# Hybrid conv / differential-attention trunk with MoE: order of the first loads, ScalarE's first table, and the place of the output bias

## The chip, the cores and the metric
One core of one Trainium2 chip. The metric is the device time of one launch in microseconds, median of several runs. The profile shows one execution, whose own time stands beside its span.

## The reference, cut to what matters
```python
for i in range(2):                          # layer 0: conformer_conv, layer 1: diff_attention
    x = x + mixer(rms_norm(x, norm1_g[i]))
    x = x + hierarchical_moe(rms_norm(x, norm2_g[i]), ...)   # 32 experts, group top-1, expert top-2

def conformer_conv(h, w_in, b_in, dw, dw_b, ln_g, ln_b, w_out, b_out):
    u = h @ w_in + b_in                     # (512,1024) @ (1024,2048)
    a, g = jnp.split(u, 2, axis=-1)
    u = a * jax.nn.sigmoid(g)
    u = causal_depthwise_conv(u, dw) + dw_b # 31 taps, each channel by itself
    u = jax.nn.silu(layer_norm(u, ln_g, ln_b))
    return u @ w_out + b_out                # (512,1024) @ (1024,1024)
```
x is 1 x 512 x 1024 float32, and so are all parameters and the output. An expert has three weight matrices of 2 MB each.

## The kernel before, in words
One program gives each engine its own instruction list; the lists meet at semaphores. x lives in `x_res` as 4 row tiles of 128 x 1024. Weights come in "units" of 2 MB (two DMAs of 1 MB, all issued by SP) into a ring of 6 buffers, and in the MoE into four more areas.

SP's list begins with the four x tiles (`L403`), the first norm gain (`L405`), units 0 and 1 (first halves of the two column groups of `w_in`, `L316` inside `mix_unit`), then six small loads into `chan_rows`: the 31 rows of the depthwise taps (`L409`), three vectors of one row (`L411`), the input bias as two rows (`L412`), and `b_out` (`L413`). Then come units 2 and 3 (the other halves of `w_in`), 4 and 5 (`w_out`), and small parameters of later stages. After that SP waits: MoE units 0 and 1 may be loaded once four groups of `w_in` columns are multiplied (`glu_ready` 4), two more at `glu_ready` 8, then at `mix_ready` 4, `mix_ready` 8 and so on.

GpSimd's list begins with constants, one after the other, and ends that part with `consts_ready` (`L508`). ScalarE, VectorE and TensorE wait for it. ScalarE (`L625`, `L626`, `L631`) then makes the row norms of the four x tiles: square and sum, root, scale. TensorE transposes the scaled tile (`L1168`), and VectorE multiplies by the gain into `hT` (`L830`). TensorE next waits for all six small loads, transposes `chan_rows` (36 rows, `L1189`), VectorE copies the result to `chan` (`L845`) and counts `chan_taken`. Only then does TensorE start the `w_in` product (`L1180`).

The convolution runs over 8 groups `ct` of 128 channels. For each, TensorE makes 16 accumulating matmuls (the profile counts 32 pieces), ScalarE the gate's sigmoid (`L646`), VectorE the gated product (`L853`). Taps 0 to 11 are multiplied by ScalarE (`L659`) and summed by GpSimd (11 adds, `L518`), taps 12 to 30 go to VectorE (`L870`, `L873`), and VectorE joins both sums (`L881`, `L882`) into `uT`, which lies in `area2`. On ScalarE the gate of group ct+1 stands after the seventh tap product of group ct. Layer-norm sums (`L1195`) come from TensorE, the rest of the layer norm is on VectorE and ScalarE.

`mix_out` multiplies `uT` by `w_out` in 8 pieces of output (2 column halves x 4 row tiles), 8 matmuls each (16 pieces in the profile, `L1231`). For layer 0 each ends with one more matmul, ones times `b_out` (`L1234`), that adds the bias. VectorE adds each result to `x_res` (`add_mix`, `L902`); from the fifth on, norm, transposes and router logits follow for the row tile.
Of the kernel before, what the change touches and what calls it, by code (L numbers as in the profile page):

```python
# [27 lines left out]
ALU = mybir.AluOpType  # L28
ACT = mybir.ActivationFunctionType
# [36 lines left out]
def trunk(nc, x, norm1_g, norm2_g, conv_w_in, conv_b_in, conv_dw, conv_dw_b, conv_ln_g, conv_ln_b,  # L66
# [11 lines left out]
    with ctx:  # L78
# [50 lines left out]


        consts_ready, params_loaded, x_loaded = sem("consts_ready"), sem("params_loaded"), [sem(f"x_loaded{t}") for t in range(NT)]
        gain_loaded, route_loaded = sem("gain_loaded"), sem("route_loaded")
# [12 lines left out]
        tap_made, tap_added, conv_done, sq_done = sem("tap_made"), sem("tap_added"), sem("conv_done"), sem("sq_done")  # L145
        stats_ready, ln_var, ln_std, ln_x, ln_done = sem("stats_ready"), sem("ln_var"), sem("ln_std"), sem("ln_x"), sem("ln_done")
        mix_ready, mix_taken = sem("mix_ready"), sem("mix_taken")

# [62 lines left out]
        chan_rows = area3[0:TAPS + 5, 0:D]  # L211
        b_out = area3[0:1, 3072:3072 + D]
        PAD = TAPS - 1
# [98 lines left out]
        def _(sp):  # L312
# [89 lines left out]
            for t in range(NT):  # L402
                sp.dma_start(x_res[:, t, :], x[0, t * P:(t + 1) * P, :]).then_inc(x_loaded[t], 16)  # L403
                if t == 0:
                    sp.dma_start(norm_g[:, 0, :], norm1_g[0].rearrange("(h p j) -> p h j", h=2, j=4)).then_inc(gain_loaded, 16)  # L405
            mix_unit(0, cols_dram(w_in, 0))
            mix_unit(1, cols_dram(w_in, D))

            sp.dma_start(chan_rows[0:TAPS, :], conv_dw[0]).then_inc(params_loaded, 16)  # L409
            for r, vec in enumerate((conv_dw_b, conv_ln_g, conv_ln_b)):  # L410
                sp.dma_start(chan_rows[TAPS + r:TAPS + r + 1, :], vec).then_inc(params_loaded, 16)  # L411
            sp.dma_start(chan_rows[TAPS + 3:TAPS + 5, :], conv_b_in[0].rearrange("(r n) -> r n", r=2)).then_inc(params_loaded, 16)  # L412
            sp.dma_start(b_out, conv_b_out).then_inc(params_loaded, 16)  # L413
            mix_unit(2, cols_dram(w_in, 512))
# [56 lines left out]
        def _(pool):  # L471
# [3 lines left out]
            def link(ins):  # L475
# [3 lines left out]
                pool.wait_ge(pool_chain, linked[0])  # L479

            link(g.memset(ones[:], 1.0))
            link(g.memset(eps[:], EPS))
            for half in range(2):
# [24 lines left out]
            g.memset(step_count[:], 0.0).then_inc(consts_ready, 1)  # L508


            k = 0
# [96 lines left out]
        def _(act):  # L608
# [8 lines left out]

            act.wait_ge(consts_ready, 1)

# [192 lines left out]
        def _(dve):  # L812
# [44 lines left out]
            for ct in range(NC):  # L857
# [4 lines left out]
                for k, w in enumerate(range(POOL_TAPS, TAPS)):  # L862
                    acc = sums[k % 2]
                    dst = uT[:, ct, :] if w == TAPS - 1 else acc
                    if k >= 2:
                        dve.wait_ge(dve_taps, k0 + k - 1)
                    elif ct >= 1:
                        dve.wait_ge(conv_done, ct)
                    if k < 2:
                        ins = v.tensor_scalar(acc, ub[:, w:w + T], chan[:, ct, w:w + 1],  # L870
                                              chan[:, ct, TAPS:TAPS + 1] if k == 0 else 0.0, ALU.mult, ALU.add)
                    else:
                        ins = v.scalar_tensor_tensor(dst, ub[:, w:w + T], chan[:, ct, w:w + 1], acc, ALU.mult, ALU.add)  # L873
                    ins.then_inc(dve_taps, 1)
# [19 lines left out]

            def add_mix(l):

                for n in range(2):
# [260 lines left out]
        def _(pe):  # L1158
# [25 lines left out]
            for t in range(NT):  # L1184
                transpose_xn(N_PRE[0], t)
            pe.wait_ge(params_loaded, 16 * 6)
            R = TAPS + 5
            for ct in range(NC):
                last = nc.tensor.transpose(bank[5][:, ct * R:(ct + 1) * R], chan_rows[:, ct * P:(ct + 1) * P], ident[0:R, 0:R])  # L1189
            last.then_inc(chan_ready, 1)  # L1190


            def stats(ct):
                pe.wait_ge(sq_done, ct + 1)
                mm(bank[4][:], ones[:], uT[:, ct, :], start=ct == 0, stop=ct == NC - 1)  # L1195
                return mm(bank[5][:], ones[:], sq_ct[:, ct, :], start=ct == 0, stop=ct == NC - 1)

            pe.wait_ge(xt_taken, 8)
            pe.wait_ge(chan_taken, 1)
            for ct in range(NC):  # L1200
# [7 lines left out]
                last = project(bank[2 * (ct % 2) + 1][:], w_chunks(ug), hT, cols)  # L1208
                last.then_inc(glu_ready, 1)
                if ct >= 3:  # L1210
                    stats(ct - 3)
# [3 lines left out]

            def mix_out(l, n0, src, bias):

# [3 lines left out]
                for n in range(2):  # L1221
                    for t in range(NT):
# [4 lines left out]
                        for c in range(NC - 1 if k < ahead[l] else 0, NC):  # L1227
                            if k == 0:

                                pe.wait_ge((ln_done, oT_done)[l], c + 1)  # L1230
                            last = mm(dst[:], src[:, c, t * P:(t + 1) * P], w_chunks(n0 + n)[:, c, :],  # L1231
                                      start=c == 0, stop=c == NC - 1 and not bias)
                        if bias:
                            last = mm(dst[:], ones[0:1, :], b_out[:, n * 512:(n + 1) * 512], start=False, stop=True)  # L1234
                        last.then_inc(mix_ready, 1)
# [140 lines left out]

            mix_out(0, 4, uT, True)
            route(0)
# [111 lines left out]
            for h, g, e in attention_steps():  # L1490
# [49 lines left out]
                if h is not None:  # L1540
                    v_half(h, 1)
            mix_out(1, n0 + 6, oT, False)
            route(1)
# [25 lines left out]
```

## Time and profile before
| | |
|---|---|
| median of 3 runs | 1679.39 us (1675.87, 1679.39, 1686.95) |
| the profiled execution | 1679.18 us, span 1677.3 us |
| TensorE busy | 1391.7 us, 83% |
| VectorE, ScalarE, GpSimd busy | 459.1, 333.1, 276.7 us |
| DMA | 473.12 MB, mean 282 GB/s |

The profiled execution's time is its span and 1.9 us around it. Times within the profile count from the start of the span. An engine's name with a q (SPq) is its sequencer: there DMAs are issued.

### The profile page before, as it was taken

The numbers are of one execution on the slowest core, as the hardware profiler recorded it, in microseconds if no ns is written. First come the engines' busy times: TensorE is split into PE (matmuls) and PEld (weight loads), VectorE is DVE, ScalarE is ACT, GpSimd is POOL, SyncE is SP. The second block draws the span as 40 slices with busy tenths as digits, with TensorE's granted clock in tenths as the row PEclk, the third lists the DMA queues.
The fourth block names the chain that finished last, engine by engine and source line by source line (L and its number), as shares of the span: only waits on it lengthen the run. The fifth ranks groups of instructions, "written<-read, shape, count | busy, mean of one in ns | idle before, by whom it ended". The sixth has DMA issues, their size and how long they took to land.

```text
span 1677.3 us, 16737 instructions
## 1 busy us (share of the span) xinstructions
PE 1391.7 (83%) x5868; PEld 623.2 (37%) x5868; DVE 459.1 (27%) x868; ACT 333.1 (20%) x629; POOL 276.7 (16%) x380
## 2 busy tenths in 40 slices
PE   4996596998778788887599999996998778778783
PEld 2442144333223232232365675644333223223231
DVE  1699714111011010110444454424111011011012
ACT  3466311110000000000334444421100000000000
POOL 1688200211111111111000000000121111111110
PEclk9998698999999999999699999996999999999997
DMA  9122015899999999999700400326899999999994
GB/s 340 25 100 100 1 67 234 345 363 419 420 421 420 420 420 419 418 417 352 269 1 1 150 1 23 129 83 239 357 382 420 421 420 420 419 419 412 419 410 183
DMA packets 91248, 473.12 MB, mean 282 GB/s; under 512 B 19675, under 2 KB 19675, under 8 KB 40260
## 3 DMA queue, kind: packets, MB, share of 16 engines
q1 hardware_dynamic: 78500, 443.12, 65.2%
q0 software_dynamic: 10400, 16.82, 2.7%
q10 hardware_dynamic: 2304, 12.58, 1.9%
q8 instruction: 28, 0.46, 0.1%
q14 instruction: 16, 0.13, 0.0%
HBM read 466.43 MB, written 23.33 MB: 292 GB/s over the span
## 4 chain that ended last, share of the span: by engine, by line
PE 48%; DMA 34%; DVE 8%; POOL 4%; SPq 3%; issue 3%; ACT 2%; ACTq 0%; POOLq 0%; DVEq 0%
DMA ring<-in_moe_w 31%; PE banks L1287 19%; PE banks L1397 5%; PE banks L1231 5%; POOL scratch L518 4%; PE banks L1304 3%; PE banks L1426 3%; SPq L316 2%; PE banks L1180 2%; DVE banks L873 2%; PE banks L1486 1%; PE banks L1441 1%; DMA area<-y_dram 1%; DMA area<-in_conv_b_out 1%; PE banks L1468 1%
## 5 line engine op out<-in xcount | busy, mean ns | idle before, releaser
L1287 PE MATMUL banks<-ring,scratch 128*64 128x512 f32 x1984 | 498.2, 653 | 145.8 <-DMA ring<-in_moe_w 134.0
L1287 PEld LDWEIGHTS banks<-ring,scratch 128*64 128x64 f32 x1984 | 159.1, 149 | 481.2 <-issue 481.2
L1015 DVE COPY scratch<-banks 128x256 f32<-128x256 f32 x65 | 27.6, 425 | 799.9 <-PE banks L1295 799.9
L1304 PE MATMUL banks<-ring,scratch 128*64 128x512 f32 x1008 | 230.2, 598 | 3.0 <-DVE scratch L1015 3.0
L687 ACT ACTIVATE scratch<-banks 64x512 f32<-64x512 f32 x65 | 38.2, 588 | 598.1 <-PE banks L1287 598.1
L536 POOL COPY at_out<-rows_out 128x1 int32 (+1 forms) x64 | 11.6, 181 | 698.1 <-ACT scratch L691 698.1
L518 POOL TENSOR_TENSOR scratch<-scratch 128x512 f32<-128x512 f32 x88 | 111.8, 1271 | 61.3 <-ACT scratch L659 50.0
L1397 PE MATMUL banks<-hT,ring 128*128 128x512 f32 x256 | 117.9, 604 | 0.9 <-DVE hT L830 0.9
L1180 PE MATMUL banks<-hT,ring 128*128 128x512 f32 x256 | 113.0, 602 | 0.7 <-issue 0.7
L1304 PEld LDWEIGHTS banks<-ring,scratch 128*64 128x64 f32 x1008 | 68.1, 136 | 117.3 <-issue 110.3
L1231 PE MATMUL banks<-ring,area 128*128 128x512 f32 x200 | 91.3, 609 | 10.6 <-ACT area L669 9.6
L691 ACT ACTIVATE scratch<-banks 128x512 f32<-128x512 f32 x65 | 38.8, 597 | 284.4 <-PE banks L1304 284.4
L873 DVE SCALAR_TENSOR_TENSOR banks<-scratch,chan,banks 128x512 f32<-128x512 f32 x128 | 85.0, 750 | 0.0
L659 ACT ACTIVATE scratch<-scratch,chan 128x512 f32<-128x512 f32 x96 | 66.7, 718 | 48.3 <-POOL scratch L518 34.5
L539 POOL DMA_INDIRECT y_dram<-scratch,at_out x64 | 65.3, 1020 | 56.5 <-POOL at_out L536 56.5
L1180 PEld LDWEIGHTS banks<-hT,ring 128*128 128x128 f32 x256 | 49.4, 194 | 63.0 <-issue 63.0
L546 POOL MEMSET scratch<- 128x512 f32 x4 | 2.1, 524 | 425.3 <-DVE x_res L902 425.2
L528 POOL DMA_INDIRECT scratch<-xn_dram,at_in x60 | 63.1, 1051 | 53.8 <-POOL at_in L525 48.5
L1397 PEld LDWEIGHTS banks<-hT,ring 128*128 128x128 f32 x256 | 46.2, 189 | 49.4 <-issue 46.9
L1426 PEld LDWEIGHTS banks<-ring,hT 128*128 128x128 f32 x512 | 59.0, 192 | 3.8 <-issue 3.8
L1231 PEld LDWEIGHTS banks<-ring,area 128*128 128x128 f32 x200 | 37.6, 194 | 61.0 <-issue 56.1
L1426 PE MATMUL banks<-ring,hT 128*128 128x128 f32 x512 | 59.6, 275 | 0.0
(208 smaller groups left out, 1142.6 us busy)
## 6 DMA issues: line engine op xcount, KB each, us to landing
ring<-in_moe_w SPq DMA_DIRECT2D x374, 1024.0 KB, 16.7
area<-in_moe_w SPq DMA_DIRECT2D x12, 1024.0 KB, 11.1
ring<-in_attn_w_qkv SPq DMA_DIRECT2D x12, 1024.0 KB, 10.8
ring<-in_conv_w_in SPq DMA_DIRECT2D x8, 1024.0 KB
area<-y_dram ACTq DMA_DIRECT2D x8, 1024.0 KB, 8.0
ring<-in_conv_w_out SPq DMA_DIRECT2D x4, 1024.0 KB, 12.9
xn_dram<-area ACTq DMA_DIRECT2D x8, 512.0 KB, 2.7
hT<-in_moe_w SPq DMA_DIRECT2D x4, 1024.0 KB, 7.6
```

Of the source, the lines that this page charges most:

```text
L518: g.tensor_tensor(pacc[ct % 2], pacc[ct % 2], tap[(k - 1) % TAP_BUFS], ALU.add).then_inc(tap_added, 1)
L528: g.indirect_dma_start(out=xe[s], out_offset=None, in_=xn_dram[l][:, :], in_offset=bass.IndirectOffsetOnAxis(ap=at_in[:, s:s + 1], axis=0) ...
L539: g.indirect_dma_start(out=y_dram[l][:, :], out_offset=bass.IndirectOffsetOnAxis(ap=at_out[:, s:s + 1], axis=0), in_=y_sb[s], in_offset=No ...
L659: a.activation(dst, u_buf[ct % 2][:, w:w + T], ACT.Copy, scale=chan[:, ct, w:w + 1]).then_inc(tap_made, 1)
L691: a.activation(y_sb[s], bank[6 + s][:], ACT.Copy).then_inc(sems["y_taken"], 1)
L873: ins = v.scalar_tensor_tensor(dst, ub[:, w:w + T], chan[:, ct, w:w + 1], acc, ALU.mult, ALU.add)
L1180: last = mm(dst, w[:, c, cols], src[:, c, :], start=start and c == 0, stop=stop and c == NC - 1)
L1231: last = mm(dst[:], src[:, c, t * P:(t + 1) * P], w_chunks(n0 + n)[:, c, :], start=c == 0, stop=c == NC - 1 and not bias)
L1287: last = mm(bank[2 + s][q * SLOTS:(q + 1) * SLOTS, :], xeT[s][:, j, h, :], w[:, c, :], start=c == 0, stop=c == NC - 1)
L1304: last = mm(bank[6 + s][q * SLOTS:(q + 1) * SLOTS, :], hidT[s][:, j, :], w2c[:, j, q * 512:(q + 1) * 512], start=j == 0, stop=j == 3)
L1397: last = mm(qk_bank[c][:], w_chunks(u)[:, k, (h % 4) * P:(h % 4 + 1) * P], hT[:, k, :], start=k == 0, stop=k == NC - 1)
L1426: last = mm(v_bank[:, t * P:(t + 1) * P], hT[:, k, t * P:(t + 1) * P], w_chunks(u)[:, k, (h % 4) * P:(h % 4 + 1) * P], start=k == 0, stop= ...
```

## The change
- SP loads the parameters ahead of units 0 and 1, not behind them. The 31 tap rows come as 16 and 15 rows; each of the five vectors comes as 16 parts of 64 numbers. Then SP waits until unit 1 has landed, loads the output bias broadcast to 128 partitions (`b_wide`, in `area2`), and only then units 2 to 5.
- TensorE no longer transposes `chan_rows` ahead of the `w_in` product but after its first group (`columns()`), and waits for `chan_taken` only at group 3.
- ScalarE no longer waits for all of GpSimd's constants but for `eps` alone, which GpSimd now writes first, and runs one root of `eps` before anything else.
- GpSimd adds `b_wide` to each tile of `x_res` once the tile's norm is taken (4 additions of 128 x 1024), ahead of its first tap sum. The bias matmul of `mix_out` is gone. VectorE waits for `bias_added` before the last two taps of group 0 and in `add_mix`.

```diff
@@ SP
+            for lo, hi in ((0, 16), (16, TAPS)):
+                sp.dma_start(chan_rows[lo:hi, :], conv_dw[0, lo:hi]).then_inc(params_loaded, 16)
+            parts = lambda ap: ap.rearrange("r (a n) -> r a n", a=16)
+            for r, vec in enumerate((conv_dw_b, conv_ln_g, conv_ln_b, conv_b_in[:, 0:D], conv_b_in[:, D:2 * D])):
+                sp.dma_start(parts(chan_rows[TAPS + r:TAPS + r + 1, :]), parts(vec)).then_inc(params_loaded, 16)
             mix_unit(0, cols_dram(w_in, 0))
             mix_unit(1, cols_dram(w_in, D))
-            sp.dma_start(chan_rows[0:TAPS, :], conv_dw[0]).then_inc(params_loaded, 16)
-            for r, vec in enumerate((conv_dw_b, conv_ln_g, conv_ln_b)):
-                sp.dma_start(chan_rows[TAPS + r:TAPS + r + 1, :], vec).then_inc(params_loaded, 16)
-            sp.dma_start(chan_rows[TAPS + 3:TAPS + 5, :], conv_b_in[0].rearrange("(r n) -> r n", r=2)).then_inc(params_loaded, 16)
-            sp.dma_start(b_out, conv_b_out).then_inc(params_loaded, 16)
+            loaded(sp, 1)
+            sp.dma_start(b_wide, conv_b_out.to_broadcast([P, D])).then_inc(bias_loaded, 16)
             mix_unit(2, cols_dram(w_in, 512))
@@ GpSimd
+            g.memset(eps[:], EPS).then_inc(eps_ready, 1)
             link(g.memset(ones[:], 1.0))
-            link(g.memset(eps[:], EPS))
...
+            pool.wait_ge(bias_loaded, 16)
+            for t in range(NT):
+                pool.wait_ge(xn_done, t + 1)
+                g.tensor_tensor(x_res[:, t, :], x_res[:, t, :], b_wide, ALU.add).then_inc(bias_added, 1)
@@ ScalarE
-            act.wait_ge(consts_ready, 1)
+            act.wait_ge(eps_ready, 1)
+            link(a.activation(small_at(21), eps[:], ACT.Sqrt))
@@ VectorE, taps and add_mix
+                    if ct == 0 and w >= TAPS - 2:
+                        dve.wait_ge(bias_added, NT)
...
+                if l == 0:
+                    dve.wait_ge(bias_added, NT)
@@ TensorE
-            pe.wait_ge(params_loaded, 16 * 6)
-            R = TAPS + 5
-            for ct in range(NC):
-                last = nc.tensor.transpose(bank[5][:, ct * R:(ct + 1) * R], chan_rows[:, ct * P:(ct + 1) * P], ident[0:R, 0:R])
-            last.then_inc(chan_ready, 1)
+            def columns():
+                pe.wait_ge(params_loaded, 16 * 7)
+                R = TAPS + 5
+                for ct in range(NC):
+                    last = nc.tensor.transpose(bank[5][:, ct * R:(ct + 1) * R], chan_rows[:, ct * P:(ct + 1) * P], ident[0:R, 0:R])
+                last.then_inc(chan_ready, 1)
             pe.wait_ge(xt_taken, 8)
-            pe.wait_ge(chan_taken, 1)
...
                 last.then_inc(glu_ready, 1)
+                if ct == 0:
+                    columns()
+                if ct == 3:
+                    pe.wait_ge(chan_taken, 1)
@@ mix_out
-                                      start=c == 0, stop=c == NC - 1 and not bias)
-                        if bias:
-                            last = mm(dst[:], ones[0:1, :], b_out[:, n * 512:(n + 1) * 512], start=False, stop=True)
+                                      start=c == 0, stop=c == NC - 1)
```

## Rows read from the trace of the kernel before

**Rows 1.** The page, chain that ended last: shares of the span.
```profile
PE 48%; DMA 34%; DVE 8%; POOL 4%; SPq 3%; issue 3%; ACT 2%; ACTq 0%; POOLq 0%; DVEq 0%
```

**Rows 2.** Chain in order of time, 0 to 72 us: start, length, what.
```profile
14.77 13.92 DMA area<-in_conv_b_out
28.73 1.06 PE banks L1189 x8
29.80 0.72 issue
30.52 29.97 PE banks L1180 x64
60.51 0.69 ACT scratch L646
...
61.89 1.28 POOL scratch L518
```

**Rows 3.** Timeline, 0 to 30 us: start, length, engine, what, [idle <-releaser].
```profile
4.13 1.28 ACT L625 ACT_TABLE_LOAD   x1 [4.13 <-DMA x_res<-in_x]
...
6.53 1.06 ACT L625 ACTIVATE scratch<-x_res 128x1024 f32<-128x1024 f32 x1 [1.12 <-POOL step_count L508]
...
7.70 1.28 ACT L626 ACT_TABLE_LOAD   x1
...
10.68 1.04 ACT L625 ACTIVATE scratch<-x_res 128x1024 f32<-128x1024 f32 x1
...
10.91 1.95 PE L1168 MATMUL banks<-ident,area 128*128 128x128 f32 x8 [10.91 <-ACT area L631]
...
13.89 0.25 SPq L411 DMA_DIRECT2D area<-in_conv_ln_g  x1
...
21.08 0.69 DVE L830 TENSOR_TENSOR hT<-banks,norm_g 128x512 f32<-128x512 f32 x1 [0.16 <-PE banks L1168]
...
29.83 0.46 DVE L845 COPY chan<-banks 128x288 f32<-128x288 f32 x1 [8.06 <-PE banks L1189]
```

**Rows 4.** Timeline, 44 to 70 us, same columns.
```profile
46.82 1.28 ACT L646 ACT_TABLE_LOAD   x1 [27.82 <-PE banks L1180]
48.12 0.69 ACT L646 ACTIVATE scratch<-banks,chan 128x512 f32<-128x512 f32 x1
48.84 0.75 DVE L853 SCALAR_TENSOR_TENSOR scratch<-banks,chan,scratch 128x512 f32<-128x512 f32 x1 [18.42 <-ACT scratch L646]
51.04 8.34 POOL L518 TENSOR_TENSOR scratch<-scratch 128x512 f32<-128x512 f32 x6 [44.54 <-ACT scratch L659]
...
56.03 0.25 SPq L432 DMA_DIRECT2D b_route<-in_moe_b_exp  x1
60.51 0.69 ACT L646 ACTIVATE scratch<-banks,chan 128x512 f32<-128x512 f32 x1 [4.61 <-PE banks L1180]
61.89 8.16 POOL L518 TENSOR_TENSOR scratch<-scratch 128x512 f32<-128x512 f32 x6 [2.51 <-ACT scratch L659]
68.92 0.70 DVE L881 TENSOR_TENSOR banks<-scratch,banks 128x512 f32<-128x512 f32 x1 [5.98 <-POOL scratch L518]
```

**Rows 5.** Chain in order of time, layer 0's output product and after.
```profile
213.18 1.05 PE banks L1234 x2
214.23 7.06 PE banks L1231 x16
221.29 1.05 PE banks L1234 x2
...
246.69 1.16 PE banks L1168 x8
247.85 6.87 PE banks L1231 x16
...
359.42 0.33 SPq L316
...
360.83 15.30 DMA ring<-in_moe_w
```

**Rows 6.** SP's waits, 200 to 480 us: total, times, longest.
```profile
SPq L316 <- PE banks L1234: 114.5, 2, 78.7
SPq L316 <- PE banks L1287: 102.7, 13, 11.6
```

**Rows 7.** Core by stretch: busy time and count, then PEclk, DMA share, GB/s.
```profile
0.00:19.50 19.50, 6.36 (x26) 5.19 (x27) 4.32 (x10) 12.60 (x18) 4.28 (x30) 1.00 0.91 323
20.00:28.70 8.70, 1.04 (x5) 0.64 (x3) 1.38 (x2) 0.00 (x0) 0.00 (x0) 1.00 1.05 354
8.00:20.00 12.00, 6.86 (x29) 5.69 (x30) 4.32 (x10) 9.87 (x15) 0.00 (x0) 1.00 1.04 391
30.50:35.00 4.50, 4.48 (x6) 1.92 (x7) 0.00 (x0) 0.00 (x0) 0.00 (x0) 1.00 0.95 351
35.00:60.00 25.00, 25.00 (x60) 11.13 (x59) 11.12 (x17) 6.70 (x9) 7.61 (x6) 1.00 0.51 145
```

**Rows 8.** DMA between 46.5 and 52 us: totals.
```profile
DMA packets 1127, 0.19 MB, mean 35 GB/s; under 512 B 1098, under 2 KB 1098, under 8 KB 1127
```

**Rows 9.** Tile x_res, 0 to 60 us: the four x loads.
```profile
DMA to landing us min/median/max: 3.3/6.1/7.3
```

**Rows 10.** Chain in order of time, layer 1's output product, which has no bias.
```profile
1119.21 0.95 PE banks L1168 x8
1120.16 6.87 PE banks L1231 x16
```

**Rows 11.** Tile ring, 0 to 90 us: durations min/median/max in ns, first and last start.
```profile
L316 SPq DMA_DIRECT2D ring<-in_moe_w x4: 355/426/647, 88.0 to 89.3; - x4
```

More of the change, by code:

```diff
@@ L128, in trunk @@
         ssq, std, rstd = small_at(0, NT), small_at(4, NT), small_at(8, NT)
+        eps_ready = sem("eps_ready")
         consts_ready, params_loaded, x_loaded = sem("consts_ready"), sem("params_loaded"), [sem(f"x_loaded{t}") for t in range(NT)]
@@ L146, in trunk @@
         stats_ready, ln_var, ln_std, ln_x, ln_done = sem("stats_ready"), sem("ln_var"), sem("ln_std"), sem("ln_x"), sem("ln_done")
+        bias_loaded, bias_added = sem("bias_loaded"), sem("bias_added")
         mix_ready, mix_taken = sem("mix_ready"), sem("mix_taken")
@@ L211, in trunk @@
         chan_rows = area3[0:TAPS + 5, 0:D]
-        b_out = area3[0:1, 3072:3072 + D]
+        b_wide = area2[:, 0:D]
         PAD = TAPS - 1
@@ L1214, in _, with mix_out @@
             stats(NC - 1).then_inc(stats_ready, 1)
-            def mix_out(l, n0, src, bias):
+            def mix_out(l, n0, src):
                 for n in range(2):
@@ L1375, in experts @@
                         down(o, 0, unit(n1 + 2), j + 1).then_inc(o["y_ready"], 1)
-            mix_out(0, 4, uT, True)
+            mix_out(0, 4, uT)
             route(0)
@@ L1541, in _ @@
                     v_half(h, 1)
-            mix_out(1, n0 + 6, oT, False)
+            mix_out(1, n0 + 6, oT)
             route(1)
```

## Prediction
> **What bounds the kernel now.** I read the page's chain first: TensorE has 48% of it and DMA 34% [rows 1], so no one engine bounds the whole, and the question is which wait ends last in the two stages that the change touches. Next, the chain in order of time. It runs through the last small load, `b_out`: issued at 14.77, landed 13.92 us later, at 28.69. Only then come the transposes of `chan_rows`, VectorE's copy, and the first `w_in` matmul at 30.52 [rows 2, 3]. The norm was long ready: the last piece of `hT` ends at 21.77 [rows 3]. So the wait for parameters costs up to 8.7 us in front of the convolution. From 30.52 TensorE does two groups in 29.97 us, ScalarE's second gate follows at 60.51, and from there GpSimd's adds carry the chain [rows 2, 4]. After the convolution the output product is a pure TensorE chain: 8.11 us for one piece of output, of which 1.05 is the bias matmul [rows 5].
>
> What follows is the MoE, bound first by TensorE and, from 359 us on, by weight loads that SP issues when TensorE frees a buffer [rows 5]. SP there waits on TensorE, two long waits on the output product and 13 on the experts' first products [rows 6]. No such wait ends by itself, so what the head saves should move the whole rest forward.
>
> **Why the parameters come late.** x and units 0 and 1 are 4 x 0.524 + 4 x 1.049 = 6.29 MB. The cores' DMA moved 323 GB/s over the first 19.5 us, which is 6.30 MB [rows 7]: the bytes of units 0 and 1 are in at 19.5 us. The six small loads hold 37 rows of 4 KB, 0.15 MB, yet need another 9 us, at 16 GB/s, while all DMA engines together do 354 in that stretch [rows 7]. That looks like one of 16 engines working the rows off one by one, at about 9.2 / 37 = 0.25 us a row, beside its share of units 2 and 3. The Trainium skill gives a reason (DMA: Bandwidth & Descriptors, "Why a DMA increments its semaphore by 16 and not by 1"): a load is split over the largest number of engines up to 16 that divides its outer dimension, so 31 rows go to one engine. This trace agrees, with those 16 GB/s. By that rule the new 16 and 15 rows use 16 and 15 engines, and the vectors' 16 parts use 16.
>
> **The change part by part.**
>
> *Parameters first, TensorE's start.* The same 0.15 MB now stands ahead of units 0 and 1. At the full rate of 391 GB/s [rows 7] it costs 0.4 us. At the rate of the stretch with many small loads, 35 GB/s [rows 8], it would cost 4.3. 127 of 147 KB are full 4 KB rows, so I take 0.6. SP needs 7 issues of 0.25 us plus gaps [rows 3], about 2 us, ahead of the units; x keeps the DMA engines busy meanwhile (it is a third of the 6.3 MB), so this is hidden. Without that cover it would cost those 2 us. From the last byte to the semaphore I take 0.9 us: the quickest x load landed 3.3 us after its issue [rows 9], of which its 0.524 MB need 1.3 to 1.8 us, so start and end share 1.5 to 2.0. Units 0 and 1 are then there at 19.5 + 0.6 + 0.9 = 21.0, and TensorE starts at 21.0, not at 30.52: 9.5 us earlier. Bounds: 20.0 and 25.5.
>
> *ScalarE's early table and the shorter wait for constants.* Now a table load, a wait for GpSimd until 6.53 and a second table load of 1.28 stand in the first tile's norm [rows 3]. With the table there and only `eps` to wait for, the square starts when x arrives, at about 4.1. VectorE still needs the constants at about 6.5, so the second tile starts near 7.8 where it started at 10.68 [rows 3], 2.9 earlier, and `hT` is ready near 18.9. The weights land at 21.0. So this edit is worth nothing by itself; it is cover that keeps `hT` (21.77 before) from being 0.8 us late. Priced at 0, but without it the start would be 21.8.
>
> *The transposes of `chan_rows`.* Before, 1.06 + 0.72 us stood in front of the product. That is already in the 9.5. Now they stand between groups 0 and 1. There the clock should be at its high level, where eight transposes of the x kind take 0.95 to 1.16 us [rows 5, 10] against 1.95 at the low level [rows 3]; the small ones took 1.06 at the low level [rows 2], so I take 0.7 on TensorE's path (bounds 0.5 and 1.1).
>
> *The clock of the start.* In the first 4.5 us of the product only 6 pieces ran (some 0.8 us each), after 35 us 60 pieces in 25 us (0.42 each) [rows 7]: the low level, 1.2 GHz, then the high one, 2.4 GHz. (PEclk reads 1.00 in both rows; the pieces speak against that for the first.) Its transposes before that (6.86 us of the 12 up to 20 [rows 7]) did not bring it up. I take the same slow start; if the rise comes up to 2 us sooner or later, half of that is gained or lost, 1 us.
>
> *The first gate.* Group 0 takes 46.8 - 30.5 = 16.3 us, so `glu_ready` 1 comes at 37.3, `chan_taken` at 37.3 + 0.7 + 0.5 (the copy [rows 3]) + 0.1 = 38.6. ScalarE's table load of 1.28 us starts on `glu_ready`, as at 46.82 [rows 4]; at 4.13 a table load ran although GpSimd's wait was still open [rows 3], so it will be hidden behind `chan_taken` (if not: 1.2 us, and see the slack next). The sigmoid is then at 38.7 instead of 48.12, the gated product at 39.4, the first GpSimd add due at 41.6 instead of 51.04: 9.4 earlier.
>
> *The second gate, which carries the chain.* TensorE reaches `glu_ready` 2 at 21.0 + 29.97 + 0.7 = 51.7, against 60.49: 8.8 us earlier. GpSimd was idle 2.51 us for that gate and VectorE then 5.98 us for GpSimd [rows 4], and with both ends moved by 9.4 and 8.8 the order stays. I take **8.8 us** for the convolution. Groups 1 to 7 repeat unchanged.
>
> *GpSimd's bias additions.* SP wakes at 21.0, the 0.5 MB broadcast needs 0.4 (issue), 1.3 (at 391 GB/s) and about 1.5 us (start and end): landed at 24.3. Four additions of 128 x 1024 at twice the 1.28 us of a 128 x 512 one [rows 2] are 10.2 us: done at 34.5. Behind them on GpSimd stand only the tap adds, due at 41.6, and then 2.5 us of idle time: 9 us of cover. At 35 GB/s [rows 8] the broadcast would take 15 us, landed near 38, and the additions end at 48: 3.3 us late. VectorE's new waits for `bias_added` are over long before its last two taps of group 0, near 51; the wait in `add_mix` costs nothing.
>
> *Units 2 to 5 held back.* From 22.7 on, 8.4 MB at 354 to 391 GB/s, in by 48. Unit 3 is wanted for group 4: SP's wait for group 3's end let MoE loads go at 88.0 before [rows 11], so near 79 now. Units 4 and 5 are wanted long after that. The last of the small loads behind them on SP is issued at 56 before [rows 4] and near 65 now, still ahead of SP's wait that ends near 79. No cost; the cover is 14 us or more.
>
> *The bias matmul gone.* It is on the chain eight times, once in each piece. It took 1.05 us, and the piece after it 7.06 where after transposes it is 6.87 (layer 0 and layer 1 alike), and the transposes after it 1.16 where layer 1 without bias shows 0.95 [rows 5, 10]. So 8 x 1.05 + 7 x 0.2 = **9.8 us**. Lower bound 8 x 1.05 = 8.4. VectorE and ScalarE between the pieces have 6.87 us for under 4 us of work, so TensorE stays last.
>
> Sum: 8.8 + 9.8 = 18.6 us, 1679.2 - 18.6 = 1660.6 for the profiled execution. Its time lies 0.2 below the median of the runs, so the same holds for that: 1660.8.
>
> **The rivals.**
> 1. *Dear small loads or a late bias.* The 0.15 MB ahead of the weights at 35 GB/s [rows 8]: start at 24.7, gain 14.9, 1664.5. The late broadcast: gain 15.3, 1664.1; both together about 1667. For it speaks that small loads do run that slowly in the one stretch that has them; against it, that most bytes here come in 4 KB rows and that x covers the issues. The Trainium skill speaks on this side (DMA: Bandwidth & Descriptors): transfers under 64 KB are dominated by their descriptors, and pieces under 512 B are written by read-modify-write. No row here has 256 B pieces alone.
> 2. *The spread does not happen*: the 15 rows, or all, go to one engine again. Then that engine has up to 15 x 0.25 = 3.8 us more than the others ahead of its share of the units, and `loaded` waits for the slowest: gain 15, 1664.4; with all 36 rows' worth on one engine 9 us late, gain 9.8, 1669.6. No row shows such a split of rows or parts, for it or against it; that x, with 128 rows, comes at nearly the full rate of all engines [rows 7] makes me hold the spread for likely.
> 3. *The gain is taken back*: clock phases in the MoE or weight loads that do not move forward. With only one of the two gains kept, 1669 to 1670. Against it: every wait of SP there is on TensorE [rows 6].
> 4. *Slower.* The one mechanism is GpSimd's queue: everything in the convolution hangs on the tap adds, and the bias additions now stand ahead of them behind SP, a landing and a broadcast. It costs 1 us for each us that the bias lands after 34.5 and outweighs the gain from 53 on; slower by 1% from about 70. At the lowest rate in sight it lands at 38, so this needs a broadcast three times slower still. At 75 us: 1679.2 - 18.6 + 40 = 1701.
>
> **How the numbers follow.** The forecast has a chance of 55%, rival 1 18%, rival 2 10%, rival 3 12%, rival 4 5%. About 1% is what a measurement of this kernel can tell from no change (the three runs lie 0.7% apart). 1% is 16.8 us, so that line lies at 1662.6, only 2 us above the forecast. Of the forecast's 55%, the clock and the scatter of the runs put about 10 behind the line; rivals 1 to 3 lie behind it by 1.5 us or more, and the same scatter puts about 10 of their 40 before it. So: faster by over 1% 0.55, within 1% 0.40, slower 0.05. Range: down to 1653 (TensorE starts at 20.0, the clock rises early, and 5 us of scatter), up to 1671 (rivals 1 to 3 with a little scatter). It leaves out rival 4 and the far ends of the others, less than 2 in 10.
>
> **What would show it.** `L1180` begins at 21 (20 to 25.5) and no longer waits for a parameter; `L1189` after the first 32 pieces; GpSimd's four additions between 24 and 35, with tap adds from 41.6; second gate near 51.7; 16 `L1234` pieces gone and output pieces every 6.9 us; x tile 2 squared near 7.8; MoE weights' first wait on SP 18 us earlier and the same total DMA. Wrong would be: the first product waiting on `ring` beyond 23; GpSimd waiting on `b_wide` after 34; a clock that stays at the low level in group 1.

## The result and the profile after

| | before | after |
|---|---|---|
| median | 1680.36 us (4 runs, 1675.87 to 1686.95) | 1665.59 us (4 runs, 1663.20 to 1667.35) |
| profiled execution | 1679.18 us, span 1677.3 | 1667.35 us, span 1665.6 |
| ratio | | 0.9915, 95% interval 0.9889 to 0.9941 |

The change saves 14.8 us, 0.85%; 18.6 were forecast. The two profiled executions lie only 11.8 us apart: that of after was the slowest of its four runs. So two things are to be explained: what the head and the output product gave, and where the profiles lost more than the medians.

The chain in order of time of after, first 75 us; compare [rows 2]:

```profile
8.14 13.65 DMA ring<-in_conv_w_in
21.79 0.14 issue
21.93 16.41 PE banks L1193 x32
38.33 0.62 PE banks L1209 x8
38.95 13.94 PE banks L1193 x32
52.90 0.02 issue
52.92 0.69 ACT scratch L655
...
54.29 1.28 POOL scratch L526
```

The parameters are gone from the chain. It now runs through units 0 and 1, which land at 21.8, and TensorE starts at 21.93 (30.52 before). The transposes of `chan_rows` stand after group 0 and cost 0.62. The second gate comes at 52.92 (60.51 before). The timeline of after shows the rest of the head, with [rows 3, 4]:

```profile
4.32 1.06 ACT L634 ACTIVATE scratch<-x_res 128x1024 f32<-128x1024 f32 x1 [2.03 <-DMA x_res<-in_x]
...
18.07 0.69 DVE L839 TENSOR_TENSOR hT<-banks,norm_g 128x512 f32<-128x512 f32 x1 [0.16 <-PE banks L1181]
21.81 0.37 SPq L416 DMA_DIRECT2D area<-in_conv_b_out  x1
21.93 16.41 PE L1193 MATMUL banks<-hT,ring 128*128 128x512 f32 x32 [3.90 <-DMA ring<-in_conv_w_in]
...
26.39 9.23 POOL L517 TENSOR_TENSOR x_res<-x_res,area 128x1024 f32<-128x1024 f32 x4 [20.02 <-DMA area<-in_conv_b_out]
...
42.63 8.34 POOL L526 TENSOR_TENSOR scratch<-scratch 128x512 f32<-128x512 f32 x6 [7.00 <-ACT scratch L668]
```

`hT` ends at 18.76, 3.2 us ahead of the weights. The four bias additions end at 35.62 and GpSimd then idles 7.00 us, so they are hidden.

The chain through the output product and into the router, after, with [rows 5]:

```profile
230.76 0.95 PE banks L1181 x8
231.72 6.87 PE banks L1248 x16
...
248.69 0.70 DVE x_res L915
...
252.32 1.98 PE banks L1181 x8
254.30 3.26 PE banks L1265 x16
...
258.13 3.56 PE banks L1265 x16
...
278.06 5.96 PE banks L1188 x8
...
285.43 13.95 PE banks L1302 x64
```

and the same stretch of before:

```profile
267.13 0.70 DVE x_res L902
...
270.76 1.23 PE banks L1168 x8
271.98 1.71 PE banks L1250 x16
...
274.03 1.91 PE banks L1250 x16
...
292.09 4.77 PE banks L1175 x8
...
298.27 13.95 PE banks L1287 x64
```

Most output pieces take 6.87 us. The last addition to `x_res` begins at 248.69 instead of 267.13: 18.4 us are saved there, nearly all that was forecast. But the first expert begins at 285.43 instead of 298.27, only 12.8 us earlier. In between, the same transposes take 1.98 us instead of 1.23, the same 16 logit pieces 3.26 and 3.56 instead of 1.71 and 1.91, and the 8 filler pieces that the kernel has there anyway 5.96 instead of 4.77. The rows by stretch say why (the columns are those of [rows 7]); first after, then before:

```profile
251.60:252.30 0.70, 0.05 (x1) 0.00 (x0) 0.67 (x2) 0.67 (x1) 0.00 (x0) 0.86 1.05 445
252.30:262.00 9.70, 9.68 (x44) 9.47 (x44) 1.38 (x2) 1.28 (x1) 0.00 (x0) 0.50 0.99 398
```
```profile
270.80:276.30 5.50, 5.47 (x44) 5.22 (x44) 1.29 (x2) 1.28 (x1) 0.00 (x0) 1.00 1.01 384
```

The same 44 pieces ran at a granted clock of 0.50, which is 1.2 GHz, and at 1.00, which is 2.4 GHz. Just before them TensorE waits for the last row tile's norm. Timeline of after, TensorE:

```profile
252.32 1.98 PE L1181 MATMUL banks<-ident,area 128*128 128x128 f32 x8 [0.68 <-DVE hT L839]
```

The question for the experiments was whether the change brings the low clock about. Their texts call two answers theory A (where the clock falls differs from execution to execution) and theory B (it falls there because the output product now ends without bias matmuls). A "filler" is a matmul by the identity whose result nobody reads.

### The profile page after: what moved, and what is told of

Same layout as the page of the kernel before. It is cut to its first block, busy times and chain, and to the rows that moved or that the text cites. A ratio compares the mean times of both kernels' runs of the same rounds, so it can differ in the third digit from the quotient of the medians.

```text
span 1665.6 us, 16714 instructions
## 1 busy us (share of the span) xinstructions
PE 1386.0 (83%) x5852; PEld 625.3 (38%) x5852; DVE 459.0 (28%) x868; ACT 332.0 (20%) x629; POOL 285.9 (17%) x384
## 4 chain that ended last, share of the span: by engine, by line
PE 48%; DMA 34%; DVE 8%; POOL 4%; issue 3%; SPq 2%; ACT 2%; ACTq 0%; POOLq 0%; DVEq 0%
DMA ring<-in_moe_w 32%; PE banks L1302 19%; PE banks L1412 5%; PE banks L1248 5%; POOL scratch L526 4%; PE banks L1319 3%; PE banks L1441 3%; SPq L318 2%; PE banks L1193 2%; DVE banks L884 2%; PE banks L1501 2%; PE banks L1456 1%; DMA area<-y_dram 1%; PE banks L1265 1%; PE banks L1483 1%
## 5 line engine op out<-in xcount | busy, mean ns | idle before, releaser
L1248 PE MATMUL banks<-ring,area 128*128 128x512 f32 x200 | 90.0, 608 | 10.6 <-ACT area L678 9.6
## 6 DMA issues: line engine op xcount, KB each, us to landing
ring<-in_attn_w_qkv SPq DMA_DIRECT2D x12, 1024.0 KB, 13.6
```

## The experiments

They ran in three groups: e0 to e2 and e6, then e3 to e5 and e7, then e8 to e11. Each ratio is to the kernel before in the same group (its medians 1681.24, 1679.18 and 1681.84 us), with its 95% interval.

| run | median us | ratio | interval |
|---|---|---|---|
| e0 changed kernel again | 1664.75 | 0.9912 | 0.9889 to 0.9936 |
| e1 loads and table only | 1671.57 | 0.9936 | 0.9913 to 0.9959 |
| e2 bias only | 1670.45 | 0.9937 | 0.9914 to 0.9960 |
| e6 changed + filler | 1659.47 | 0.9867 | 0.9842 to 0.9892 |
| e3 late table | 1662.40 | 0.9898 | 0.9876 to 0.9919 |
| e4 no hold | 1662.09 | 0.9893 | 0.9868 to 0.9918 |
| e5 no spread | 1670.11 | 0.9935 | 0.9911 to 0.9958 |
| e7 more fillers | 1661.35 | 0.9895 | 0.9873 to 0.9916 |
| e8 before + filler | 1679.55 | 0.9985 | 0.9970 to 1.0001 |
| e9 filler, no hold | 1657.55 | 0.9860 | 0.9841 to 0.9880 |
| e10 as e6 | 1660.29 | 0.9879 | 0.9860 to 0.9899 |
| e11 as e7 | 1660.89 | 0.9882 | 0.9866 to 0.9899 |

What the profiles add, read the same way in each: start of the first `w_in` matmul; then for each layer the time from the start of VectorE's last addition to `x_res` until the first expert's matmul, and how long after that addition the granted clock fell.

```
run      w_in starts  layer 0: stage, clock falls after   layer 1: stage, clock falls after
before     30.52         31.1      10.3                      36.9       3.8
after      21.93         36.7       3.4                      36.9       3.9
e0         22.98         35.3       4.0                      35.3       4.0
e1         22.07         35.3       4.1                      36.9       3.9
e2         30.57         36.7       3.4                      36.9       3.9
e3         21.73         33.7       6.0                      36.9       3.8
e4         22.73         35.2       3.9                      36.9       3.7
e5         27.82         35.3       4.0                      35.3       4.3
e6         22.93         33.6      10.8                      33.5      10.6
e7         22.21         32.4      10.0                      32.0      11.0
e8         30.22         33.7      10.8                      33.5      10.7
e9         22.50         33.1       9.5                      32.0      11.1
e10        22.18         33.5      10.7                      33.3      10.3
e11        23.30         32.4      10.8                      32.2      10.9
```

### The halves of the change, and the clock (e0, e1, e2, e6)

e0 is the changed kernel. 

> The changed kernel once more, unedited. Theory A (what is missing from the forecast was lost to the granted clock after the output product of layer 0): where the clock falls is not the same in each execution, so a new profile may show the logits of layer 0 at either speed (16 pieces in 1.71 us or 3.3 to 3.6 us); the median stays at 0.991 of before. Rival theory B (the fall belongs to this kernel, because its output product ends without the bias matmuls): the fall comes within 4 us of the last output piece again, and the experts begin 13 us earlier than before, not 18.

Measured: 0.9912 again. The clock fell 4.0 us after the addition, and the first expert begins at 285.64, 12.6 us earlier than before, which are theory B's numbers.

e1 puts the bias back on TensorE; GpSimd's additions and the waits for them are taken out:
```diff
-            sp.dma_start(b_wide, conv_b_out.to_broadcast([P, D])).then_inc(bias_loaded, 16)
+            sp.dma_start(b_out.rearrange("r (a n) -> r a n", a=16), conv_b_out.rearrange("r (a n) -> r a n", a=16)).then_inc(bias_loaded, 16)
...
+                        if bias:
+                            last = mm(dst[:], ones[0:1, :], b_out[:, n * 512:(n + 1) * 512], start=False, stop=True)
```


> Load order and early table kept, bias back on TensorE as a matmul. By the sum: 8.2 us faster than before (ratio 0.995), the first w_in matmul near 21.9, output pieces every 8.11 us again. Theory B adds: with the bias matmuls the clock stays high through the logits (1.71 us for 16 pieces), so all of the head's 8 us arrives at the experts. Theory A: the clock after the last output piece can go either way.

e2 is the kernel before with `b_wide`, GpSimd's additions and the waits for them, but the old order of loads:
```diff
-            sp.dma_start(b_out, conv_b_out).then_inc(params_loaded, 16)
+            sp.dma_start(b_wide, conv_b_out.to_broadcast([P, D])).then_inc(bias_loaded, 16)
```


> The kernel before with the output bias alone moved to GpSimd. By the sum: 9.8 us faster (ratio 0.994) at the last output piece, TensorE still starting between 28 and 30.5. Theory B: the clock falls within 4 us of the last output piece and 4 to 5.6 us are given back, so 4.5 to 6 us faster (0.997). Theory A: either.

e6 adds to the changed kernel, in `mix_out` ahead of the last row tile's transposes:
```diff
+                stay_warm(2, (bank[4], bank[0])[l])
                 transpose_xn(N_MOE[l], NT - 1)
```


> The changed kernel with two identity matmuls of 512 columns (4 pieces) in each layer's wait between the last output piece's logits and the last row tile's transposes. They cost about 1.0 us a layer (1.7 us of work in a gap of 0.7). Theory B: they keep the clock high through transposes and logits, so the stage runs 4 us shorter in each layer: 5 to 6 us faster than the changed kernel in all. Theory A: no systematic effect on the clock, 2 us slower at most.

Measured: e1 is 10.8 us faster than before by its ratio (forecast 8.2), e2 10.6 (forecast 9.8), both inside their intervals of 4 us. Their sum is 21 us, that of the whole change 14.8; with such intervals that is no proof of a loss when both are joined. In the profiles e1's last addition begins at 257.76, 9.4 earlier than before, and e2's at 255.73, 11.4 earlier. Both contain the same 1.7 us: the last layer-norm sums ran at the low clock in before (3.67 us on the chain) and at the high one in e1, e2 and after (2.00 in after). Counted once, the halves make 19.1 us, where the whole change has 18.4. For e2 theory B expected only 4.5 to 6 us; its clock fell 3.4 us after the addition, and still it gained 10.6, which points to the runs of before losing time there too.

The clock fell within 4.1 us in e1 too, which has all eight bias matmuls. Its rows by stretch:

```profile
257.80:261.50 3.70, 3.24 (x27) 3.09 (x28) 2.00 (x4) 2.59 (x4) 1.05 (x2) 1.00 0.67 250
261.50:271.00 9.50, 9.50 (x44) 9.24 (x44) 1.38 (x2) 1.28 (x1) 0.00 (x0) 0.52 0.99 397
```

So theory B, that the fall belongs to a kernel without bias matmuls, is refuted. The fall is the usual case: of the eight profiles without an added filler, all but that of before show it in layer 0, and all eight in layer 1, where no kernel has a bias. It could have been read in the trace of before, whose row for layer 1's transposes and logits says 0.50:

```profile
1140.90:1150.60 9.70, 9.70 (x44) 9.37 (x44) 1.38 (x2) 1.28 (x1) 0.00 (x0) 0.50 0.99 392
```

Among these eight the profile of before is the exception, by 2.5 to 5.6 us in layer 0, and that brings the two profiles closer together than the medians.

And the fall can be put off until the logits are done. With two matmuls in TensorE's wait of 0.7 us the stretch is full and stays at 2.4 GHz; e6:

```profile
250.40:260.50 10.10, 10.10 (x74) 8.85 (x73) 3.33 (x6) 3.88 (x5) 1.05 (x2) 1.00 0.89 329
```

e6 beats e0 beside it by 5.3 us, the 5 to 6 of theory B; but its reason was wrong, so the number does not speak for it. Theory A's "no systematic effect" falls as well. What the profiles show is a third thing: the fall is usual after that wait, in kernels with and without the bias matmuls, and with the wait filled the clock stays high past the logits. Why the profile of before escaped, with the same wait (0.46 us) as e1, stays open. Nor is such a wait enough by itself. Ahead of layer 1's output product TensorE waits longer, and the clock stays at 2.4 GHz for another 39 us, until 1129.33. Timeline of after, TensorE:

```profile
1090.11 17.40 PE L1248 MATMUL banks<-ring,area 128*128 128x512 f32 x40 [0.94 <-DVE area L1164]
```

What follows this wait are matmuls of 512 columns; what follows the other are matmuls of 128 and 36 columns. No run tells whether that is the difference.

### The parts of the head (e3, e4, e5)

e3:
```diff
-            act.wait_ge(eps_ready, 1)
-            link(a.activation(small_at(21), eps[:], ACT.Sqrt))
+            act.wait_ge(consts_ready, 1)
```


> The changed kernel with ScalarE's old beginning (waits for all of GpSimd's constants, no root of eps ahead). Forecast's theory: hT is ready at 21.8 instead of 18.8, the weights land between 21.9 and 22.9, so TensorE starts at the same time and the kernel is as fast as the changed one (within 0.5 us). Rival: the early table is what brought the start forward; then the start falls back by up to 3 us.

TensorE starts at 21.73; the chain there is the last piece of `hT` (0.70 from 20.98), and unit 1's last part landed at 21.53, so `hT` and the weights are level. Nothing is lost: 1662.40 beside e4's 1662.09; no unedited run of the changed kernel stands in this group. The early table is worth nothing here, as forecast.

e4:
```diff
-            loaded(sp, 1)
             sp.dma_start(b_wide, conv_b_out.to_broadcast([P, D])).then_inc(bias_loaded, 16)
```


> The changed kernel without SP's wait for unit 1 ahead of the bias broadcast and units 2 to 5. If the DMA engines work in the order of issue, units 0 and 1 land as before (TensorE starts at 22 to 23), the bias lands about 2 us sooner, and the time is that of the changed kernel. Rival: loads issued later take bandwidth from units 0 and 1 once there are more of them; then TensorE starts later, by up to the 6 us that 8.9 MB behind would cost if they shared evenly from their issue on.

TensorE starts at 22.73, within the 21.93 to 23.30 of the kernels with the hold, and GpSimd's additions begin at 23.99 instead of 26.39. Timeline of e4, GpSimd:

```profile
23.99 9.25 POOL L516 TENSOR_TENSOR x_res<-x_res,area 128x1024 f32<-128x1024 f32 x4 [17.59 <-DMA area<-in_conv_b_out]
42.44 8.36 POOL L525 TENSOR_TENSOR scratch<-scratch 128x512 f32<-128x512 f32 x6 [9.20 <-ACT scratch L667]
```

So the later loads take nothing from units 0 and 1 that shows, and holding them back brings nothing. The Trainium skill states it (DMA: Bandwidth & Descriptors, "Queues, rings and completion order"): on each DMA engine a queue's descriptors are consumed in the order of the ring. This trace agrees: unit 1 landed at 22.60, among the 21.53 to 23.16 of the kernels with the hold.

e5 keeps the parameters first but in their old shapes (the input bias stays two rows of their own), and TensorE waits for six loads instead of seven:
```diff
-            for lo, hi in ((0, 16), (16, TAPS)):
-                sp.dma_start(chan_rows[lo:hi, :], conv_dw[0, lo:hi]).then_inc(params_loaded, 16)
+            sp.dma_start(chan_rows[0:TAPS, :], conv_dw[0]).then_inc(params_loaded, 16)
...
-                sp.dma_start(parts(chan_rows[TAPS + r:TAPS + r + 1, :]), parts(vec)).then_inc(params_loaded, 16)
+                sp.dma_start(chan_rows[TAPS + r:TAPS + r + 1, :], vec).then_inc(params_loaded, 16)
```


> The changed kernel with the parameters still ahead of the units but in their old shapes: 31 rows in one load, each vector as one row. Theory (one DMA engine takes all 36 rows, about 0.25 us each): that engine comes to its share of units 0 and 1 some 8 to 9 us late, TensorE starts near 30, and the head's gain is gone: 8 us slower than the changed kernel. Rival (rows were slow before only because units 2 and 3 shared the engines): start near 22.5, no loss.

TensorE starts at 27.82, 5.3 us later than the mean of the nine profiles with the parameters spread and the early table (22.5), and the time is 1670.11, 7.7 to 8.0 us behind e3 and e4 beside it. Rows by stretch of e5:

```profile
20.00:24.00 4.00, 0.00 (x0) 0.00 (x0) 0.00 (x0) 0.00 (x0) 0.00 (x0) 1.00 0.33 125
24.00:28.00 4.00, 0.18 (x1) 0.21 (x2) 0.00 (x0) 0.00 (x0) 0.00 (x0) 1.00 0.06 22
```

From 24 to 28 us the DMA share is 0.06, one sixteenth: one engine is still at work on its part of the units, the other fifteen have nothing left. This shows what the forecast argued from 16 GB/s, that the rows all go through one engine; the rival, that units 2 and 3 slowed them, is out, since those are held back here. The start is lost by 5.3 us, not 8: a row costs less than 0.25 us (4 KB at the 22 GB/s of that row is 0.19, an estimate). That the medians show the expected 8 us is therefore in part luck. In the profile another 2.9 us go between layer 0's first expert and layer 1's last addition (841.7 us for 838.8 in e4); their cause is open.

### More filler, and the best version (e7 to e11)

e7 is e6 with more filler:
```diff
             def route(l):
+                stay_warm(6, bank[7])
                 pe.wait_ge(picks_done, l + 1)
...
+                stay_warm(8, bank[7])
                 pe.wait_ge(hot_done, 2 * l + 1)
...
-                stay_warm(4, bank[7])
+                stay_warm(2, bank[7])
```


> The changed kernel with the filler of the tail, and also fillers in TensorE's two waits of the routing stage (6 identity matmuls in a gap of 6.3 us, 8 in one of 7.9), while the four at its end, 6.2 us at the low clock, become two. If the clock stays high through the stage and the gather of the rows lands near 280, the experts begin 2 to 3 us earlier in each layer than with the tail's filler alone: 4 to 6 us faster than that, near 1654. Rival: the clock falls anyway in the remaining gaps, the fillers then delay TensorE's short matmuls (6 of them are 10 us at the low clock, in a gap of 6.3), and it is slower than with the tail's filler alone by up to 8 us.

e8 is the kernel before with e6's line. 

> The kernel before with the tail's filler alone (two identity matmuls in each layer, as in the filler run before). In six of seven profiles without a filler the clock fell 3 to 6 us after layer 0's last output piece, and in all of them after layer 1's; the one exception was the profile of before. Theory A now: the fall is a matter of TensorE's waits there and not of the bias matmuls, so the filler helps the kernel before as well: both layers' logits at 1.71 us for 16 pieces, 3 to 6 us faster than before (ratio 0.997). Theory B (only the kernel without bias matmuls loses its clock): 2 us at most, from layer 1 alone.

e9 is e6 without the hold. 

> The changed kernel with the tail's filler and without SP's wait ahead of the bias and of units 2 to 5. The hold showed no effect by itself, so this should be as fast as the filler alone: 20 to 22 us faster than before (0.987 to 0.988). Rival: the hold does protect the start now and then; then 1 to 2 us slower than with the hold.

e10 is e6, e11 is e7, on the same chip beside them.

> The changed kernel with the tail's filler again, for a comparison on one chip with the next two: 20 to 22 us faster than before (0.987).

> The tail's filler and the fillers in the routing waits again. The profile showed the experts of each layer beginning 2 us earlier than with the tail's filler alone, the medians of two different jobs showed no gain. If the 2 us a layer are real: 4 us faster than the run beside it. Rival: nothing, since the loads of the experts set the pace from the fifth expert on and the gain is taken back there.

e8 gains 2.5 us (-0.2 to 5.0 by its interval): below theory A's 3 to 6, just over theory B's 2, so it does not separate them. Its layer 1 stage is 3.4 us shorter than before's, its layer 0 stage 2.5 us longer than the one of before's profile. How often the kernel before keeps its clock in layer 0 would need more profiles of it, but each run's mean granted clock is on record. In the 17 runs of before beside e8 it was 0.926 to 0.928 in the eight fastest (up to 1680.37 us) and 0.921 to 0.925 in the nine others (1681.84 to 1689.00); the profile of before has 0.928. In layer 0 the clock was low for 17.1 us in before's profile and for 30.7 in after's. The 13.6 us between them at half clock are 0.004 of a run (an estimate), about the distance between the two groups. So the scatter of before goes with the clock, and it would fit that before escapes in about half of its runs. It is not shown, since these figures do not say in which stage the clock was low. With the filler, in e8, all 12 runs have 0.927 to 0.929.

e7 was expected near 1654 and came at 1661.35. e7 and e11 shorten the stage by 1.1 to 1.5 us a layer against e6 and e10, less than the 2 to 3 expected: two matmuls of filler now end before the gathered rows land, and TensorE waits for those. Chain of e7:

```profile
277.57 2.77 DMA scratch<-xn_dram,rows_in
...
280.38 1.13 PE banks L1295 x4
```

The medians (1660.29 for e10, 1660.89 for e11) show none of it, as e11's rival said. The profiled e11 started 1.1 us later than e10, and from layer 1's first expert to the end e7 and e11 take 502.7 and 502.4 us, e6 and e10 500.5 and 500.6: 2 us are given back there. That the loads of the weights take them is not shown.

What filler is worth is less certain than e6 makes it look. e7 stands beside e3 and e4, which are changed kernels without filler, on another chip than e6. In the profiles its two stages together are 6.2 and 7.7 us shorter than theirs, but its median is only 1.1 and 0.7 us lower, within the scatter of the runs. The last group holds no changed kernel without filler. So the effect on the clock is shown in 12 stages, and the 5.3 us by one pair of medians.

The best median is e9's, 0.9860: the changed kernel with the filler and without the hold, 1657.55 us, 24 us faster than before. Its distance to e10 (2.7 us) is within the intervals, so the hold can't be said to cost anything.

## Why the prediction was right, and where its sizes were off

- *The bound.* Right. The wait for the parameters stood between `hT` and the product, and nearly all of what the head saved was still there at 249 us.
- *Parameters first, TensorE's start.* Forecast 21.0, 9.5 us earlier. Measured 21.93, and 22.5 on the mean of nine profiles (21.93 to 23.30): 8.0 us. The forecast's saving was 1.5 us too large here, in two steps. The base: the forecast let units 0 and 1 land at 19.5 + 0.9 = 20.4, but by the semaphore updates of the traces unit 1's last part landed at 20.77 in before, 20.87 in e8 and 21.11 in e2. The price of the parameters: with them ahead it landed at 21.79 in after and at 22.4 on the mean of the nine, so they cost 1.5 us and not 0.6. In the profile of after the 6.43 MB of x, parameters and units were in only near 21.0 (306 GB/s over 21 us), where the sum had 20.1. Part of that lies in a term priced at nothing, SP's issues hidden behind x: the first unit is issued at 6.10 instead of 3.15, and when x runs out at about 9 us there is a dip. First after, then before:

```profile
9.00:10.50 1.50, 0.85 (x4) 0.45 (x3) 1.35 (x3) 1.27 (x3) 0.00 (x0) 1.00 0.89 266
```
```profile
9.00:10.50 1.50, 0.00 (x0) 0.00 (x0) 0.16 (x1) 1.17 (x2) 0.00 (x0) 1.00 1.02 384
```

At 384 GB/s the missing bytes are 0.5 us (an estimate).
- *ScalarE's early table.* Priced at 0, shown by e3. The sentence "without it the start would be 21.8" was exact (21.73), but with the weights landing at 21.53 and not 21.0 it is hardly late at all.
- *Transposes and clock of the start.* 0.62 for 0.7; group 0 took 16.41 for 16.3, and 15.41 to 17.04 in the experiments, as the clock rose sooner or later: the ±1 us allowed.
- *The second gate and the convolution.* Forecast 8.8, measured 7.6 at the gate (52.92 for 60.51). In the groups that follow another 0.6 were lost: VectorE's last join of the sums begins at 172.76 instead of 179.71, 6.95 earlier. After the second gate GpSimd has eight short waits in after and three in before; e0 and e2 to e5 repeat the eight, e1, whose bias is not on GpSimd, has the three. So "groups 1 to 7 repeat unchanged" was not quite so; why is open. The last layer-norm sums, which ran at 2.4 GHz in after and at 1.2 in before, gave 1.7 back: luck, since no term of the forecast has it.
- *GpSimd's bias additions.* Hidden, as forecast. The broadcast landed 4.5 us after its issue, not 3.3, and an addition of 128 x 1024 took 2.31 us, not twice the 1.28 of a 128 x 512: done at 35.6 for 34.5.
- *Units 2 to 5 held back.* No cost, shown by e4, and no use.
- *The bias matmul gone.* Forecast 9.8. In the profiles the last addition moved by 18.44 and the layer norm's end by 8.63: 9.8. e2 has 10.6 by its ratio, with an interval of 4 us either way.
- *The gain kept to the end.* The steps above sum to 18.4 at the last addition of layer 0, with 1.7 from the clock in it; 16.8 without. From there to the first expert the profile of after gives back 5.6 us, to layer 1's last addition another 1.2 (840.0 us for 838.9), and from layer 1's first expert to the end nothing (503.2 for 503.3): no wait for weights took the gain. The median says 14.8, with 4 us of interval either way. The 2 us between 16.8 and that are not settled. The term that I left out is the clock in the router: rival 3 named "clock phases in the MoE", but the place is the wait at the end of the output product. The profiles without filler lose 2.5 to 5.6 us there against that of before, whose runs may do without the fall in about half the cases (see e8); that would explain the 2 us, but isn't shown.
- *The rivals.* The median of 1665.59 lies nearer to the 1664.1 to 1664.5 of rivals 1 and 2 than to the forecast's 1660.8, but their mechanisms did not come. Small loads at 35 GB/s would start TensorE at 24.7; it started at 21.93 to 23.30. The late bias would end GpSimd's additions at 48; they ended at 35.6. No engine came 3.8 us late; e5 shows what that looks like. What is missing was lost after the output product.

The chances were fair: the forecast lay 2 us beyond the 1% line, the median fell 2 us short of it.

## What to carry to other kernels

Look at the shape of small loads ahead of a bound start. Here 31 rows in one load, and vectors as single rows, went through one DMA engine, and what stood behind them on that engine waited; as 16 and 15 rows and as 16 parts they did not hold anything up for long. Putting them first without changing their shape gives back most of what it brings (e5: TensorE starts 2.7 us earlier than before instead of 8.0).

Read repeated stages against each other before a forecast. Layer 1 of before already showed the router at half clock; one profile of layer 0 was taken for the rule. A profile pair can differ by 4 to 5.6 us through the clock of one stage alone, so a gain of 1% is to be read from medians, and the profile only says where.

A wait of 0.7 us in TensorE's chain, with short matmuls behind it, can cost more than its length. Filler in it kept the clock up in both kernels and is cheap to try; its worth in the medians was 5.3 us in one pair, 2.5 in the kernel before and about 1 beside e3 and e4.

## What the hardware showed that was not expected

- The granted clock fell 3.4 to 6.0 us after the last output piece's addition began in 15 of 16 such stages without filler, after TensorE had worked at 2.4 GHz for 35 us or more with no such wait, and then waited 0.5 to 0.7 us ahead of short matmuls; with 4 more pieces in the wait it fell in none of 12 before 9.5 us. A wait of 0.94 us ahead of 512-column matmuls (after, 1090.11) brought no fall.
- With one DMA engine at work the core's DMA share read 0.06, and 22 GB/s (e5, 24 to 28 us).
- GpSimd adds 128 x 1024 float32 in 2.31 us and 128 x 512 in 1.27.
